# Column blocks of eight with bias tables in the same order, and the head order of the attention stage

## The chip, the cores and the metric

One core of one Trainium2 chip runs the whole program. The metric is the device time of one execution in microseconds (us). An instruction is named by its engine: PE is TensorE (matmuls and transposes), DVE is VectorE, ACT is ScalarE, POOL is GpSimd, and SP only issues DMAs. All data is float32.

## The reference: what is computed

512 tokens of width 1024 on a grid of 8 rows and 64 columns pass two layers. A layer is:

```
proj = x @ w_in                      # six blocks of 512: diff q, k, v and neighbourhood q, k, v
8 differential heads:  s_m = q_m k_m^T / sqrt(32) + t5_bias[bucket(key - query)],  m = 0, 1
                       o = (softmax(s_0) - lam * softmax(s_1)) @ v;  rms_norm(o) * g * (1 - lam_init)
8 neighbourhood heads: s = q k^T / 8 + rpb[row offset, column offset], only the 16 nearest columns
                       o = softmax(s) @ v
x = layer_norm(alpha * x + concat(o) @ w_out)
x = layer_norm(alpha * x + peer_ffn(x))      # product-key retrieval over 16384 experts
```

The result is x, (1, 512, 1024). With 8 grid rows the neighbourhood window covers all rows, so a neighbourhood head is limited in columns alone.

## The kernel before

`build` makes constants (`setup`), then runs a hardware loop over the two layers: `project`, `attend`, and three stages for the PEER part (`route`, `gates`, `experts`), which the change does not touch. A last block stores x.

**Token order.** x lies in SBUF as four tiles of 128 tokens (`per["x"][:, tt, :]`). Tile tt holds 16 grid columns of all 8 rows; inside it the column is the slow index and the row the fast one (`column_tokens`). Queries and keys have this order in every later stage.

**Project** (L361 on). Twelve half blocks j of `w_in` are loaded by SP into two buffers, split by ACT (L446) and DVE (L480) into a high and a low part, and multiplied on PE in three passes (L236 to L238); two result tiles n = 2j, 2j+1 come from each. ACT moves each tile out (L455, L463). The first eight tiles (q and k of the differential heads) also go to DRAM by SP (`store`, L412), and ACT may move tile n out only when the store of tile n-2 has landed. SP also copies the neighbourhood bias table 128 times to a DRAM scratch (L406) and loads the T5 table `tb` (L435): row p of `tb[:, h]` is the T5 bias of head h over 560 (row, column) offsets, cut so that the 512 entries that a query tile needs are one window of it. They come out of a scratch, filled once by ACT's queue in `setup` (L314).

**Attend** (L539 on). A unit u is one head for one query tile: 4 tiles of 16 heads, 64 units. A differential unit has two maps of 512 keys, a neighbourhood unit one map of 256. Each unit passes
- PE: scores into one of 4 PSUM banks (L864), three units ahead;
- DVE `maxima`: adds the bias, writes the negated sum to SBUF and keeps its minimum, in one instruction per map (L773);
- ACT: exponential with the row sum (L726);
- DVE `mix`, one unit behind: reciprocal, factor, and the weighted difference of the two maps (L784, L786, L789), differential units only;
- PE `turn`: transposes into the one bank Tb (L875); ACT `move`: Tb to SBUF (L736), two units behind; PE `values`: times v into O (L890), two units behind.

Every engine has its own instruction list, written out by `with_tails`: `unit(u)` for each u, and after unit 16*qt + slot the pieces of the **tail** of query tile qt. The tail reads O, normalises the differential heads (read_diff, gain), transposes them (turn_na, turn_diff), multiplies by w_out in four parts of 8 matmuls (mul_0 to mul_3, L934), adds to x (add_0, add_1, L833) and does the layer norm (stats, norm; L274 to L286). The slots decide where in the lists of the next tile's units these pieces stand. Only half of w_out fits: after mul_1, SP loads the other half (L645), and mul_2 waits for it. Limits between units: PB = 3 buffers of probabilities (maxima of u waits for turn of u-3), SB = 4 score banks, one bank Tb.

The order of heads is `mixed_order`: differential heads 0 to 5 (first tile) or 0 and 1 (others), then neighbourhood and differential heads in turn, then the neighbourhood heads left. The bias reads in L773 are

```
bias = tb[:, h, first:first + T].rearrange("p (r c) -> p c r", r=GR)
keys, bias = NKEYS, nb[:, EDGE[qt], h - NDH, :, :].rearrange("p r c -> p c r")
```

so the elements read one after the other lie 64 (T5) or 32 (neighbourhood) elements apart.

## Time and profile before

| | us |
|---|---|
| median of 3 runs (3435.12 to 3437.94) | 3437.25 |
| profiled execution, device time | 3439.33 |
| profiled execution, span | 3437.4 |
| PE busy | 3186.5 |
| DVE busy | 2554.2 |
| ACT busy | 1213.5 |
| POOL busy | 1083.8 |

The span is that of the recorded instructions; the device time holds 1.9 us more around it. Busy times are sums over the execution; engines overlap. A share of busy time says nothing of one stage, so the stages that the change touches are read from windows of the trace.

### The profile page before, as it was taken

The numbers are of one execution on the slowest core, as the hardware profiler recorded it, in microseconds if no ns is written. First come the engines' busy times: TensorE is split into PE (matmuls) and PEld (weight loads), VectorE is DVE, ScalarE is ACT, GpSimd is POOL, SyncE is SP. The second block draws the span as 40 slices with busy tenths as digits, with TensorE's granted clock in tenths as the row PEclk, the third lists the DMA queues.
The fourth block names the chain that finished last, engine by engine and source line by source line (L and its number), as shares of the span: only waits on it lengthen the run. The fifth ranks groups of instructions, "written<-read, shape, count | busy, mean of one in ns | idle before, by whom it ended". The sixth has DMA issues, their size and how long they took to land. (4 is left out here: it accounts for less than half of the span.)

```text
span 3437.4 us, 48720 instructions
## 1 busy us (share of the span) xinstructions
PE 3186.5 (93%) x16726; PEld 2820.0 (82%) x16726; DVE 2554.2 (74%) x5128; ACT 1213.5 (35%) x1716; POOL 1083.8 (32%) x684
## 2 busy tenths in 40 slices
PE   7988799899899999999889877998998999999997
PEld 6865489899899999988777664898998999999886
DVE  3186488899688878878832773898996888887787
ACT  2254233344333333333322551333443333332332
POOL 0020036500255545533200200474003555454332
PEclk9988899999999999999989898999999999999998
DMA  7541224446899999989675312244549999998995
GB/s 263 135 112 47 98 76 149 158 183 237 314 347 347 348 327 335 320 301 356 239 219 128 102 35 100 87 169 143 220 194 353 350 349 336 329 343 294 328 352 212
DMA packets 333656, 801.99 MB, mean 233 GB/s; under 512 B 39072, under 2 KB 195232, under 8 KB 298944
## 3 DMA queue, kind: packets, MB, share of 16 engines
q1 hardware_dynamic: 258736, 527.47, 44.7%
q0 software_dynamic: 73728, 268.47, 20.8%
q10 hardware_dynamic: 1040, 4.19, 0.3%
q8 instruction: 74, 1.21, 0.2%
q14 instruction: 78, 0.64, 0.1%
HBM read 711.45 MB, written 94.90 MB: 235 GB/s over the span
## 5 line engine op out<-in xcount | busy, mean ns | idle before, releaser
L236 PE MATMUL o_bank<-v_hi,w_hi 128*128 128x512 f32 x1536 | 599.6, 390 | 15.5 <-DVE w_lo L1580 15.5
L173 POOL DMA_INDIRECT g_ring<-in_peer_u,g_idx x256 | 361.6, 1412 | 796.6 <-DVE g_ring L183 747.3
L238 PE MATMUL o_bank<-v_hi,w_lo 128*128 128x512 f32 x1536 | 600.3, 391 | 0.0
L237 PE MATMUL o_bank<-v_lo,w_hi 128*128 128x512 f32 x1536 | 600.3, 391 | 0.0
L173 POOL DMA_INDIRECT g_ring<-in_peer_v,g_idx x256 | 372.3, 1454 | 505.9 <-DVE x_sb L191 449.9
L236 PE MATMUL h_bank<-x_hi,ws_hi 128*128 128x384 f32 x1152 | 385.7, 335 | 4.5 <-PEq L1248 4.5
L238 PE MATMUL h_bank<-x_hi,ws_lo 128*128 128x384 f32 x1152 | 385.7, 335 | 0.0
L237 PE MATMUL h_bank<-x_lo,ws_hi 128*128 128x384 f32 x1152 | 385.3, 334 | 0.0
L1565 DVE TENSOR_TENSOR v_lo<-v_raw,v_hi 128x2048 fp32r<-128x2048 f32 x128 | 292.8, 2288 | 123.8 <-ACT v_hi L1500 123.8
L183 DVE SCALAR_TENSOR_TENSOR g_ring<-g_ring,x_sb 128x1024 f32<-128x1024 f32 x256 | 306.4, 1222 | 99.3 <-DMA g_ring<-in_peer_u,g_idx 98.4
L1500 ACT CAST v_hi<-v_raw 128x2048 fp32r<-128x2048 f32 x128 | 244.9, 1913 | 375.2 <-PE o_bank L238 341.5
L191 DVE SCALAR_TENSOR_TENSOR x_sb<-g_ring,g_h,x_sb 128x1024 f32<-128x1024 f32 x256 | 328.3, 1282 | 58.3 <-DMA g_ring<-in_peer_v,g_idx 40.7
L236 PEld LDWEIGHTS o_bank<-v_hi,w_hi 128*128 128x128 f32 x1536 | 289.4, 188 | 74.6 <-issue 16.1
L238 PEld LDWEIGHTS o_bank<-v_hi,w_lo 128*128 128x128 f32 x1536 | 289.2, 188 | 60.6
L237 PEld LDWEIGHTS o_bank<-v_lo,w_hi 128*128 128x128 f32 x1536 | 289.4, 188 | 59.0
L236 PE MATMUL r_bank<-x_hi,ws_hi 128*128 128x384 f32 (+1 forms) x768 | 275.5, 359 | 12.5 <-DVE x_lo L267 12.5
L1180 POOL TENSOR_TENSOR ws_lo<-ws_raw,ws_hi 128x2048 fp32r<-128x2048 f32 x44 | 203.2, 4618 | 242.7 <-ACT ws_hi L1028 242.7
L237 PE MATMUL r_bank<-x_lo,ws_hi 128*128 128x384 f32 (+1 forms) x768 | 272.4, 355 | 0.0
L238 PE MATMUL r_bank<-x_hi,ws_lo 128*128 128x384 f32 (+1 forms) x768 | 272.2, 354 | 0.0
L1309 DVE TENSOR_SCALAR onehot<-iota,key1T,gateT 128x128 f32<-128x128 f32 x768 | 214.2, 342 | 33.3 <-PE g_bank L1340 26.0
L1340 PE MATMUL g_bank<-onehot 128*128 128x128 f32 x1536 | 208.5, 279 | 26.5 <-DVE onehot L1312 26.5
L1340 PEld LDWEIGHTS g_bank<-onehot 128*128 128x128 f32 x1536 | 199.5, 194 | 35.6 <-DVE onehot L1312 33.4
(190 smaller groups left out, 6118.5 us busy)
## 6 DMA issues: line engine op xcount, KB each, us to landing
ws_raw<-in_uT SPq DMA_DIRECT2D x128, 1024.0 KB
v_raw<-in_peer_v SPq DMA_DIRECT2D x128, 1024.0 KB
gates_T<-gate_stage SPq DMA_DIRECT2D x12, 4096.0 KB, 12.6
g_raw<-gates_T SPq DMA_DIRECT2D x128, 384.0 KB
w_raw<-in_w_in SPq DMA_DIRECT2D x24, 1024.0 KB, 6.3
ws_raw<-hidden_T SPq DMA_DIRECT2D x56, 384.0 KB
w_out_half<-in_w_out SPq DMA_DIRECT2D x8, 2048.0 KB, 8.1
ws_raw<-in_peer_wq SPq DMA_DIRECT2D x16, 1024.0 KB
```

Source lines behind the costliest of these rows:

```text
L173: nc.gpsimd.indirect_dma_start(out=tail.ring[n % RING][:, :], out_offset=None, in_=table.rearrange("l e d -> (l e) d"), in_offset=bass.Ind ...
L183: nc.vector.scalar_tensor_tensor(row, row, 1.0, xt, ALU.mult, ALU.mult, accum_out=tail.h[:, bass.ds(base + j, 1)]).then_inc(tail.used, 1)
L191: nc.vector.scalar_tensor_tensor(xt, tail.ring[j % RING][:, :], tail.h[:, bass.ds(base + j, 1)], xt, ALU.mult, ALU.add).then_inc(tail.used, 1)
L236: nc.tensor.matmul(out, lh, rh, start=start, stop=False)
L237: nc.tensor.matmul(out, lh, rl, start=False, stop=False)
L238: return nc.tensor.matmul(out, ll, rh, start=False, stop=stop)
L1180: nc.gpsimd.tensor_tensor(wl[n % 2][:, :, :], raw[n % 2][:, :, :], wh[n % 2][:, :, :].bitcast(F32), ALU.subtract).then_inc(lo_done, 1)
L1309: nc.vector.tensor_scalar(A[u % 2][:, t, :], iota[:, :], key1[:, bass.ds(col, 1)], gate[:, bass.ds(col, 1)], ALU.is_equal, ALU.mult)
L1340: ins = nc.tensor.matmul(bank[u % 4][:, t * NK:(t + 1) * NK], A[u % 2][:, t, :], B[u % 2][:, t, :], start=True, stop=True)
L1500: nc.scalar.copy(v_hi[k][:, :, :], v_raw[k][:, :, :]).then_inc(v_split, 1)
L1565: nc.vector.tensor_tensor(v_lo[k][:, :, :], v_raw[k][:, :, :], v_hi[k][:, :, :].bitcast(F32), ALU.subtract).then_inc(v_ready, 1)
```

## The change

- Tokens of a tile are now two blocks of 8 columns: block, then row, then column inside the block. Constants, the load of x and the store of the result follow; each of the 4 loads and 4 stores becomes two, of 64 partitions each.
- The T5 tables are laid out so that the 512 biases of a query tile lie one behind the other: SP loads the rows as before (2 DMAs instead of 8), and ACT copies them at the end of `project` (8 copies of 896 elements). The fill of the T5 scratch moves from `setup` to ACT's queue in `project` (after tile pair j = 1), so it is done in each layer. The neighbourhood tables are built by POOL in blocks of 64 elements. L773 now reads both tables block by block.
- The copy of the neighbourhood table to DRAM becomes two DMAs with 8 as their outermost dimension (16 before).
- Every tile runs its differential heads first (units 0 to 7) and then its neighbourhood heads (8 to 15), and all slots of the tail change.
- In the tail, the squares for the norm of the heads go from DVE to ACT, the gain g is applied by ACT while it moves the transposed heads, and the layer norm takes its sum from the add and its squares from ACT in place of the two statistics instructions on DVE.

```diff
+CB = 8
+TB = TC // CB
+T5_PITCH = CB * REL + GW - CB
+T5_W = (2 * GW - TC) * GR
+T5_RAW = NDH * (T5_W - TBW) + TBW
...
-    cq = np.arange(P) // GR
+    cq = np.arange(P) // (GR * CB) * CB + np.arange(P) % CB
...
+def column_tokens(t, n, g):
+
+    return at(t, (n * TC + g * CB) * D, [[GW * D, GR], [D, CB], [1, D]])
+
+
+def block_rows(g):
+
+    return slice(g * (P // TB), (g + 1) * (P // TB))
...
-                sp.dma_start(per["x"][:, tt, :], column_tokens(a["x"], tt)).then_inc(x_in, 16)
+                for g in range(TB):
+                    sp.dma_start(per["x"][block_rows(g), tt, :], column_tokens(a["x"], tt, g)).then_inc(x_in, 16)
...
-        @block.scalar
-        def _(act):
-            act.wait_ge(vec_made, 2)
-            nc.scalar.dma_start(at(t5_scratch, 0, [[NDH * REL, P], [REL, NDH], [1, REL]]),
-                                per["t5_vec"][:, None, :].to_broadcast([P, NDH, REL])).then_inc(t5_stored, 16)
...
-            sp.dma_start(at(rpb_scratch, 0, [[GR * RPC + 1, TC], [RPC + RPW, GR], [1, NNH * DRS * RPW]]),
-                         at(a["na_rpb"], l * (NNH * DRS * RPW), [[0, TC], [0, GR], [1, NNH * DRS * RPW]]))\
-                .then_inc(rpb_copied, 16)
+            for g in range(TB):
+                sp.dma_start(at(rpb_scratch, g * (GR * CB * RPC + CB),
+                                [[CB * RPC + RPW, GR], [RPC + 1, CB], [1, NNH * DRS * RPW]]),
+                             at(a["na_rpb"], l * (NNH * DRS * RPW), [[0, GR], [0, CB], [1, NNH * DRS * RPW]]))\
+                    .then_inc(rpb_copied, 16)
...
-                    for h in range(NDH):
-                        src = at(t5_scratch, h * P * REL + (T - 1) - (TT - 1) * TC,
-                                 [[GR * REL - 1, TC], [REL - GW, GR], [1, TBW]])
-                        sp.dma_start(tb[:, h, :], src).then_inc(tab_in, 16)
-            sp.wait_ge(tab_in, 16 * NDH)
+                    rows_first = tb[:, T5_RAW:T5_RAW + NDH * TBW].rearrange("p (h w) -> p h w", h=NDH)
+                    for g in range(TB):
+                        src = at(t5_scratch, (T - 1) - (TT - 1) * TC + g * (GR * T5_PITCH - CB),
+                                 [[REL - 1, GR * CB], [TB * GR * T5_PITCH, NDH], [1, TBW]])
...
+                if j == 1:
+                    nc.scalar.dma_start(at(t5_scratch, 0, [[T5_PITCH, P], [REL, CB], [1, REL]]),
+                                        per["t5_vec"][:, None, :].to_broadcast([P, CB, REL])).then_inc(t5_stored, 16)
+                if j == HALVES - 2:
+                    act.wait_ge(tab_in, 16 * TB)
+                    for h in range(NDH):
+                        first = T5_RAW + h * TBW
+                        if h >= 1:
+                            act.wait_ge(tab_made, h)
+                        nc.scalar.copy(tb[:, h * T5_W:(h + 1) * T5_W].rearrange("p (g r c) -> p g r c", r=GR, c=CB),
+                                       blocks_of_rows(tb, first)).then_inc(tab_made, 1)
...
+def blocks_of_rows(tb, first):
+
+    whole = tb[:, first:first + TBW]
+    return bass.AP(whole.tensor, whole.offset, [whole.ap[0], [CB, T5_W // (GR * CB)], [GW, GR], [1, CB]])
...
-        ORDERS = [mixed_order(6 if qt == 0 else 2) for qt in range(TT)]
+        ORDERS = [list(range(NH))] * TT
...
-        PE_SLOTS = {"turn_na": 20, "turn_diff": 23, "mul_0": 26, "mul_1": 27, "mul_2": 30, "mul_3": 31}
-        ACT_SLOTS = {"turn_na": 22, "turn_diff": 25}
-        DVE_SLOTS = {"read_diff": 18, "read_na": 20, "gain": 21, "add_0": 30, "add_1": 35, "stats": 37, "norm": 39}
-        POOL_SLOTS = {"read_diff": 18, "stats": 37}
-        SP_SLOTS = {"mul_1": 27}
+        PE_SLOTS = {"turn_diff": 15, "turn_na": 18, "mul_0": 20, "mul_1": 21, "mul_2": 23, "mul_3": 24}
+        ACT_SLOTS = {"square": 11, "turn_diff": 16, "turn_na": 19, "spread": 26}
+        DVE_SLOTS = {"read_diff": 11, "sums": 12, "gain": 14, "read_na": 18, "add_0": 22, "add_1": 25, "spread": 27,
+                     "norm": 28}
+        POOL_SLOTS = {"sums": 12, "spread": 27}
+        SP_SLOTS = {"mul_1": 21}
...
+                if piece == "square":
+                    act.wait_ge(o_read[0], qt + 1)
+                    if qt >= 1:
+                        act.wait_ge(spread, qt)
+                    nc.scalar.activation(sq, cat[:, 0:NDH, :], ACT.Square).then_inc(squared, 1)
                 if piece in ("turn_na", "turn_diff"):
                     i = 0 if piece == "turn_diff" else 1
-                    act.wait_ge(cat_turned, 2 * qt + (2 - i))
-                    if qt >= 1:
-                        act.wait_ge(hid, 2 * qt)
-                    nc.scalar.copy(catT[:, 4 * i:4 * i + 4, :].rearrange("p a b -> p (a b)"),
-                                   tail_bank(qt, 1 - i)[:, :]).then_inc(cat_moved, 1)
+                    act.wait_ge(cat_turned, 2 * qt + (i + 1))
+                    dst = catT[:, 4 * i:4 * i + 4, :].rearrange("p a b -> p (a b)")
+                    if i == 0:
+                        act.wait_ge(rms_asked, qt + 1)
+                        nc.scalar.activation(dst, tail_bank(qt, 0)[:, :], ACT.Copy,
+                                             scale=gd[:, 0:1]).then_inc(cat_moved, 1)
+                    else:
+                        if qt >= 1:
+                            act.wait_ge(spread, qt)
+                        nc.scalar.copy(dst, tail_bank(qt, 1)[:, :]).then_inc(cat_moved, 1)
+                if piece == "spread":
+                    act.wait_ge(centred, qt + 1)
+                    nc.scalar.activation(catT[:, :, :].rearrange("p a b -> p (a b)"), x[:, qt, :], ACT.Square,
+                                         bias=mv[:, 0:1], accum_out=mv[:, 1:2]).then_inc(spread, 1)
 
...
-                        keys, first = T, (TT - 1 - qt) * TC
-                        bias = tb[:, h, first:first + T].rearrange("p (r c) -> p c r", r=GR)
+                        keys, first = T, h * T5_W + (TT - 1 - qt) * P
+                        bias = tb[:, first:first + T]
+                        by_block = lambda t: t
                     else:
                         dve.wait_ge(nb_ready, h - NDH + 1 if qt == 0 else NNH + EDGE[qt])
-                        keys, bias = NKEYS, nb[:, EDGE[qt], h - NDH, :, :].rearrange("p r c -> p c r")
-                    by_column = lambda t: t.rearrange("p (c r) -> p c r", r=GR)
-                    nc.vector.tensor_tensor_reduce(by_column(s[u % PB][:, k, 0:keys]),
-                                                   by_column(S[(before + k) % SB][:, 0:keys]), bias, -1.0,
+                        keys, bias = NKEYS, nb[:, EDGE[qt], :, h - NDH, :, :].rearrange("p g r c -> p g (r c)")
+                        by_block = lambda t: t.rearrange("p (g k) -> p g k", k=GR * CB)
+                    nc.vector.tensor_tensor_reduce(by_block(s[u % PB][:, k, 0:keys]),
+                                                   by_block(S[(before + k) % SB][:, 0:keys]), bias, -1.0,
...
-                if piece == "read_diff":
-                    dve.wait_ge(o_read[0], qt + 1)
-                    if qt >= 1:
-                        dve.wait_ge(hid, 2 * qt)
-                    chain.done(nc.vector.tensor_tensor(sq, d, d, ALU.mult))
-                    chain.wait()
+                if piece == "sums":
+                    dve.wait_ge(squared, qt + 1)
                     chain.done(nc.vector.tensor_reduce(ms[:, 0, :], sq, AX_X, ALU.add))
                     chain.wait()
                     nc.vector.tensor_scalar(ms[:, 0, :], ms[:, 0, :], 1.0 / HD, EPS, ALU.mult,
                                             ALU.add).then_inc(rms_asked, 1)
                 if piece == "gain":
                     dve.wait_ge(rms_done, qt + 1)
-                    chain.done(nc.vector.tensor_tensor(d, d, ms[:, 1, :, None].to_broadcast([P, NDH, HD]), ALU.mult))
-                    chain.wait()
-                    nc.vector.tensor_tensor(d, d, gd[:, None, :].to_broadcast([P, NDH, HD]),
+                    nc.vector.tensor_tensor(d, d, ms[:, 1, :, None].to_broadcast([P, NDH, HD]),
                                             ALU.mult).then_inc(cat_done, 1)
...
-                                                   ALU.add).then_inc(x_done, 1)
-                if piece == "stats":
+                                                   ALU.add, accum_out=st[:, i:i + 1]).then_inc(x_done, 1)
+                if piece == "add_1":
+                    dve.wait_ge(x_done, 2 * (qt + 1))
+                    nc.vector.tensor_scalar(mv[:, 0:1], st[:, 0:1], st[:, 1:2], -1.0 / D, ALU.add,
+                                            ALU.mult).then_inc(centred, 1)
+                if piece == "spread":
+                    dve.wait_ge(spread, qt + 1)
+                    nc.vector.tensor_scalar(rs[:, 0:1], mv[:, 1:2], 1.0 / D, EPS, ALU.mult,
+                                            ALU.add).then_inc(pow_asked, 1)
+                if piece == "norm":
                     dve.wait_ge(ln_in, 32)
-                    dve.wait_ge(x_done, 2 * (qt + 1))
-                    norm_stats(nc, chain, xt, st, mv, rs[:, 0:1], pow_asked)
-                if piece == "norm":
-                    norm_apply(nc, dve, chain, xt, mv, lnp[:, 0, :], lnp[:, 1, :], rs[:, 1:2], pow_done, qt + 1)
+                    dve.wait_ge(centred, qt + 1)
+                    chain.done(nc.vector.scalar_tensor_tensor(xt, xt, mv[:, 0:1], lnp[:, 0, :], ALU.add, ALU.mult))
+                    chain.wait()
+                    dve.wait_ge(pow_done, qt + 1)
+                    chain.done(nc.vector.scalar_tensor_tensor(xt, xt, rs[:, 1:2], lnp[:, 1, :], ALU.mult, ALU.add))
 
...
-                sp.dma_start(column_tokens(out, tt), per["x"][:, tt, :]).then_inc(written, 16)
-            sp.wait_ge(written, 16 * TT)
+                for g in range(TB):
+                    sp.dma_start(column_tokens(out, tt, g), per["x"][block_rows(g), tt, :]).then_inc(written, 16)
+            sp.wait_ge(written, 16 * TT * TB)
```

## Rows read from the trace of the kernel before

**Rows 1.** Window of one period: length, busy of PE, PEld, DVE, ACT, POOL; PE clock, DMA.
```profile
287.30:342.40 55.10, 45.64 (x221) 33.94 (x219) 38.38 (x92) 25.05 (x66) 3.81 (x4) 0.85 0.16 48
```
**Rows 2.** PE in time, third query tile: start, length, form, idle before.
```profile
299.23 3.60 PE L934 MATMUL Hb<-w_out_half,heads_outT 128*128 128x512 f32 x8
...
304.38 3.60 PE L934 MATMUL Hb<-w_out_half,heads_outT 128*128 128x512 f32 x8
...
316.46 5.84 PE L934 MATMUL Hb<-w_out_half,heads_outT 128*128 128x512 f32 x8 [4.51 <-DMA w_out_half<-in_w_out]
...
323.63 3.60 PE L934 MATMUL Hb<-w_out_half,heads_outT 128*128 128x512 f32 x8
...
354.55 3.79 PE L934 MATMUL Hb<-w_out_half,heads_outT 128*128 128x512 f32 x8
```
**Rows 3.** DVE groups by line and shape: count, busy us, mean ns, idle before.
```profile
L773 DVE CUSTOM_DVE_ANT_1 probs<-S,t_toeplitz 128x512 f32<-128x512 f32 x128 | 128.4, 1045 | 54.6 <-PE S L864 46.8 <-PE Tb L875 7.6
...
L773 DVE CUSTOM_DVE_ANT_1 probs<-S,na_bias 128x256 f32<-128x256 f32 x64 | 38.2, 597 | 59.5 <-PE Tb L875 59.3
...
L496 DVE SCALAR_TENSOR_TENSOR q_diff_parts<-p_bank,q_diff_parts 128x512 fp32r<-128x512 f32 x16 | 11.1, 692 | 59.3 <-ACT q_diff_parts L455 59.3
```
**Rows 4.** DVE in time, second tile: mix of one unit, next unit's first map.
```profile
242.49 0.16 DVE L784 RECIPROCAL map_factor<-rowsum 128x1 f32<-128x1 f32 x1 [0.36 <-ACT probs L726]
...
243.61 1.02 DVE L773 CUSTOM_DVE_ANT_1 probs<-S,t_toeplitz 128x512 f32<-128x512 f32 x1
```
**Rows 5.** PE in time, one differential unit at full clock, one matmul group at half clock.
```profile
239.70 1.00 PE L890 MATMUL O<-dv,probsT 128*128 128x64 f32 x8
240.54 0.60 PE L875 MATMUL Tb<-ident,probs 128*128 128x128 f32 x4
240.90 0.72 PE L864 MATMUL S<-k_diff_parts,q_diff_parts 128*128 128x512 f32 x2
241.45 0.55 PE L890 MATMUL O<-nv_half_shifted,probsT 128*128 128x64 f32 x4
...
283.63 1.81 PE L890 MATMUL O<-dv,probsT 128*128 128x64 f32 x8
```
**Rows 6.** ACT group of the squares in `experts`.
```profile
L1551 ACT ACTIVATE ws_raw<-x_sb,bn_mv 128x1024 f32<-128x1024 f32 x6 | 6.9, 1151 | 23.0 <-DVE bn_mv L1648 23.0
```
**Rows 7.** DVE in time: first map of the stage, first map of the second tile.
```profile
172.72 1.05 DVE L773 CUSTOM_DVE_ANT_1 probs<-S,t_toeplitz 128x512 f32<-128x512 f32 x1 [23.35 <-PE S L864]
...
212.61 1.06 DVE L773 CUSTOM_DVE_ANT_1 probs<-S,t_toeplitz 128x512 f32<-128x512 f32 x1 [1.39 <-PE Tb L875]
```
**Rows 8.** PE in time, end of the attention stage: last turn, last products.
```profile
377.78 0.39 PE L875 MATMUL Tb<-ident,probs 128*128 128x128 f32 x2
...
389.64 8.51 PE L934 MATMUL S<-w_out_half,heads_outT 128*128 128x512 f32 x16 [0.77 <-ACT heads_outT L750]
397.99 7.03 PE L934 MATMUL S<-t_toeplitz,heads_outT 128*128 128x512 f32 x16
```
**Rows 9.** DVE in time, last instruction of the attention stage.
```profile
409.27 1.28 DVE L286 SCALAR_TENSOR_TENSOR x_sb<-x_sb,ln_rs,ln_params 128x1024 f32<-128x1024 f32 x1 [0.53 <-POOL ln_rs L698]
```
**Rows 10.** Window in the load of x, columns as in rows 1.
```profile
10.00:12.00 2.00, 0.00 (x0) 0.00 (x0) 0.00 (x0) 0.00 (x0) 0.00 (x0) 1.00 1.03 233
```
**Rows 11.** ACT in time, start of `project` in the first and in the second layer.
```profile
13.83 1.28 ACT L260 ACT_TABLE_LOAD   x1 [13.83 <-PEq L291]
...
25.84 1.90 ACT L446 CAST w_hi<-w_raw 128x2048 fp32r<-128x2048 f32 x1 [6.87 <-DMA w_raw<-in_w_in]
...
1725.25 1.28 ACT L260 ACT_TABLE_LOAD   x1 [10.70 <-issue]
...
1733.18 1.90 ACT L446 CAST w_hi<-w_raw 128x2048 fp32r<-128x2048 f32 x1 [1.91 <-DMA w_raw<-in_w_in]
```
**Rows 12.** SP's issues at the end.
```profile
3428.16 4.39 SPq L1778 DMA_DIRECT2D out<-x_sb  x4
```
**Rows 13.** DMA issues by line: count, KB each, median us to landing.
```profile
rpb_rows<-in_na_rpb SPq DMA_DIRECT2D x2, 3840.0 KB, 16.7
```

73 lines of the change are left out of this document (39 added, 34 removed).

## The prediction

> **What bounds the kernel now.** I read the page first: PE is busy nearly all the span, but the edits lie in the load of x, `project`, `attend` and the store, so the windows come next. In `attend` [rows 1] no engine is full: of a period of 55.10 us PE is busy 45.64 and DVE 38.38. The timeline then shows what a period is made of [rows 2]. From mul_0 (299.23) to the end of mul_3 (323.63 + 3.60) it is 28.0 us, and there PE sets the pace: four blocks of eight matmuls, and a wait of 4.51 us for the second half of w_out, after which mul_2 takes 5.84 us where the others take 3.60. The other 27.3 us, to the next mul_0 at 354.55, are DVE's: mixed pairs and the DVE pieces of the tail. A saving on DVE can thus show only in the second half of a period, in the first tile, and at the end.
>
> **The map instruction.** A T5 map takes 1.045 us for 512 elements, a neighbourhood map 0.597 for 256 [rows 3]. The difference is 1.75 ns an element, the start cost 0.15 us. L496 also reads PSUM and SBUF and writes SBUF, 512 elements one behind the other, in 0.692 us. I take that for the new T5 map (-0.35) and 0.15 + 256 x 1.06 ns = 0.42 for the other (-0.18). The bounds are L496's time and no change at all. The whole is 128 x 0.35 + 64 x 0.18 = 56 us of DVE work; the next parts ask how much of it shows. The Trainium skill (Advanced Engine Details and Errata, SBUF Cachelines) says that SBUF has lines of 16 bytes and that a new line for each access is penalised; by it the 256-byte step is what costs, and the new read is free of it.
>
> **A differential unit** on DVE: mix is 242.49 to 243.61, 1.12 us [rows 4], two maps 2 x 0.61 (0.69 less the overlap with the next start), so 2.35 us; before 3.05. On PE the unit is 0.84 + 0.36 + 0.55 = 1.75 us from the starts in [rows 5]; at half clock the O group takes 1.81 in place of 1.00, and the unit about 3.5.
>
> **A period after**, with time 0 where mul_0 starts (after unit 20):
> - mul_0 to 3.4, unit 21 to 5.1, mul_1 to 8.5. DVE's add_0 stands in slot 22 and waits for mul_1, with the maps of unit 23 and mix of 22 queued behind it. PE needs that mix for turn 22, and gets it at 8.5 + 0.7 + 1.2 + 1.1 = 11.5: it idles 1.7 us.
> - Units 22 and 23 end at 13.6. The half of w_out lands as late after mul_1 as before (307.8 to 316.46, 8.65 us [rows 2]), at 17.2. The wait is 3.6 us where it was 4.51, since two units lie in front of it where three did, but one of them was late. mul_2 5.84, unit 24 1.6, mul_3 3.4: 28.0 us, as before. That half gains nothing.
> - Then add_1 and the sum to 29.0; ACT squares x, 1.15 us [rows 6] plus 0.19 for the read of the sum, behind the exponential of unit 26; DVE waits for it in `spread` until 31.6, then read_diff 0.9, both norm instructions 2.6, sums 0.9: 36.3. POOL's power (1.65) and gain: 38.7. The neighbourhood units 28 to 31 wait for DVE meanwhile, then go through Tb at some 1.1 us each: turn 31 at 41.9. Five differential units at 2.35: turn 36 at 54.2.
> - Clock: in the period before it was 0.85 of full [rows 1]. PE is now idle for about half of the stretch 29 to 42, so the first differential units behind it will meet the half clock, where PE (3.5) and not DVE (2.35) sets the unit. I add 1.8: a period of 56.0 against 55.3. Three tails lie over units: +2 us a layer. Bounds: 54.2 (-3) and three more units at half clock a tile (+12).
> So most of the DVE saving is lost: units are no longer mixed, so the DVE-heavy and the latency-bound ones do not cover each other.
>
> **The first tile** took 39.9 us (172.72 to 212.61 [rows 7]). After: eight differential units in 23.5 (18.8 by DVE; PE at half clock in the first four, POOL's building of tables beside the mixes), eight neighbourhood units at 1.1, and 3.5 for the DVE pieces in slots 11 to 14: 36. That is -4, bounds 0 and -7.
>
> **The end of the stage** took from the last turn (377.78 + 0.39) to 409.27 + 1.28 [rows 8, 9] 32.4 us, with mul_3 of the third tile and the whole differential tail behind the turn. Now both lie before it. What is left: two values 1.3, read_na 0.9, transposes and their move 1.1, the 32 matmuls 15.4 [rows 8], add and mean 1.0, square 1.3, power and scaling 1.7, last norm 1.3, signals 1: 25. That is -7, bounds -9 and -4.
>
> Attention: 2 x (+2 - 4 - 7) = **-18 us**.
>
> **Load of x.** While it runs all DMA engines are full (1.03) at 233 GB/s [rows 10]: 9.0 us for 2.1 MB. The transfers were 16 rows outermost over 128 partitions and are 8 rows outermost over 64. No row shows an outermost dimension of 8. If it changes nothing, 0; if 8 engines carry it, 18.0 us, +9.0. I take the upper end: full engines leave nothing else to give. Against it the 4 MB store of the T5 scratch leaves this place: in the first layer w_in came 12.0 us after the block's start, in the second, without that store beside it, 7.9 [rows 11]: -4.1. Net +4.9.
> **Store of x.** It runs from 3428.16 to the end of the span at 3437.4 [rows 12], 9.2 us for the same 2.1 MB. Bounds 0 and +9; I take +7, doubling all but the latency of the last.
> **Project.** The copy of the table takes 16.7 us to land [rows 13] with w_in, stores and all else of SP's queue behind it; doubled, it delays the moves of tiles n = 2, 3 and with them the split for j = 3, which has about 6 us to spare in the first layer and less in the second. The T5 store comes right behind on ACT's queue. Bounds 0 and +10 a layer, I take +1: +2. The eight copies by ACT (some 1.0 us each) lie between moves that are 5.2 us apart on an idle ACT and end before the last matmul: 0; uncovered they would be 8 a layer. Building the tables on POOL: same elements, 0.
>
> Sum against the profiled execution: 3439.3 - 18 + 4.9 + 7 + 2 = 3435.2; the median of the runs is 2.1 below that execution, so **3433 us**.
>
> The Trainium skill (DMA: Bandwidth & Descriptors, Why a DMA increments its semaphore by 16 and not by 1) says that a transfer runs on the largest number of engines up to 16 that divides the slowest dimension of both sides, 8 here. By it the forecast stands; without it, the first rival.
>
> **Rivals.**
> - Transfers as fast as before. For it: no row at 8 against it; full engines may be full with waiting. Then 9.0, 7 and 2 fall away: 3415. Chance 0.25.
> - The clock. PE idles in the neighbourhood run and is then held at half clock through most of the differential run: 1.15 us more for each of 8 to 9 units a layer: +10 a layer, 3453, slower. It decides once more than about 5 of the 20 differential units behind the tails and in the first tile beyond those I count are at half clock. For it: 0.85 mean clock in a period that had shorter gaps [rows 1]. Against: PE is full while it is slow, as in mul_2, after which it ran at 3.60 again. Chance 0.18.
> - The map stays at 1.045 us: the instruction, not its read, is slow. Then the some 21 differential units a layer that DVE paces cost 0.7 more: +15 a layer, 3463, slower. No row shows this instruction on a contiguous bias. Chance 0.07.
> - The periods come out at the full-clock sum, 54.2: 3422. Chance 0.08.
>
> **How the numbers follow.** The forecast has 0.42, with 3424 to 3443 as its own range. A measurement of this kernel tells 0.2% (7 us) from no change, so faster is below 3430. Of the forecast's chance 0.15 is faster, 0.21 the same, 0.06 slower. With the rivals: faster 0.15 + 0.23 + 0.07 = 0.45; same 0.21 + 0.02 + 0.01 = 0.24; slower 0.06 + 0.18 + 0.07 = 0.31. The range 3410 to 3456 leaves out the third rival and the edges.
>
> **What would show it.** L773 at about 0.69 and 0.42 us. First transposes of the first layer near 22 us, not 14, and the windows before them with half the DMA share. From mul_0 to mul_3's end 28 us, with 1.7 us of PE idle between unit 22's values and its turn. Periods near 56, the first tile 36, last turn to last norm 25 us. From the first store issue to the end 16 us. Wrong: a period below 53 or above 59, or loads that land as before.

## The result and the profile after

The changed kernel takes **3461.2 us** (median of four runs, 3460.4 to 3461.9) where the kernel before takes 3437.6: ratio 1.007, 95% interval 1.0057 to 1.0082. It is slower; 3433 had been forecast. The profiled executions have spans of 3459.5 and 3437.4 us, and the 22.1 us between them divide so ("attend" is from SP's first q load to the end of the last norm instruction, "project" from the start of the layer's work to that load):

| | before | after | difference | forecast |
|---|---|---|---|---|
| setup and project, layer 0 | 168.5 | 173.7 | +5.1 | +5.9 |
| attend, layer 0 | 242.0 | 244.1 | +2.1 | -9 |
| project, layer 1 | 150.3 | 154.1 | +3.8 | +1 |
| attend, layer 1 | 240.0 | 244.2 | +4.2 | -9 |
| both expert parts | | | -0.3 | 0 |
| store of x | 9.2 | 16.5 | +7.2 | +7 |

The first row looks like its forecast, but by luck. PE's first matmul with w_in stands at 27.6 us, 31.3 before, so the head of the layer is 3.7 us shorter, where 4.9 longer had been forecast; from there to the first q load it takes 146.1 us, 137.2 before, 8.9 longer, where 1 had been forecast.

The maps are as fast as forecast. The groups of DVE by line and shape, after, against [rows 3]:

```profile
L821 DVE CUSTOM_DVE_ANT_0 probs<-S,t_tables 128x512 f32<-128x512 f32 x128 | 82.8, 686 | 64.2 <-PE S L915 46.7 <-PE Tb L926 17.3
...
L821 DVE CUSTOM_DVE_ANT_1 probs<-S,na_bias 128x256 f32<-128x256 f32 x64 | 25.9, 419 | 5.2 <-PE Tb L926 5.0
```

That is 1045 to 686 ns and 597 to 419 ns, 57 to 58 us less work for DVE. The next two fences are one window each over attend of layer 0 (columns as in [rows 1]: length, busy PE, PEld, DVE, ACT, POOL, clock, DMA share, GB/s), before and then after:

```profile
168.54:410.55 242.01, 187.10 (x864) 134.92 (x864) 158.06 (x356) 100.60 (x264) 38.16 (x40) 0.84 0.26 75
```

```profile
173.66:417.75 244.09, 185.63 (x864) 134.44 (x864) 121.91 (x348) 102.15 (x276) 37.92 (x40) 0.86 0.26 75
```

DVE is busy for 36 us less, and the stage is 2 us longer. The first place where the saving is lost is the end of the first tile. PE in time, after:

```profile
216.26 1.22 PE L915 MATMUL S<-k_diff_parts,q_diff_parts 128*128 128x512 f32 x2 [5.80 <-DMA q_diff_parts<-diff_qk_parts]
217.27 0.95 PE L941 MATMUL O<-nv,probsT 128*128 128x64 f32 x4
```

PE wants the q of tile 1 and waits 5.80 us for it. SP's issues in time, after, say why it is late:

```profile
188.07 0.98 SPq L699 DMA_DIRECT2D nv_half_shifted<-nv  x1
189.09 0.60 SPq L700 DMA_DIRECT2D nv_half_shifted<-nv  x1
204.03 0.38 SPq L675 DMA_DIRECT2D w_out_half<-in_w_out  x1
204.60 0.44 SPq L703 DMA_DIRECT2D ln_params<-in_ln_g  x1
205.14 0.38 SPq L704 DMA_DIRECT2D ln_params<-in_ln_b  x1
205.57 9.66 SPq L671 DMA_DIRECT2D q_diff_parts<-diff_qk_parts  x16
```

SP stands from 189.7 to 204.03 at its wait for POOL's last table, because w_out goes into the buffer that POOL reads. POOL's row ends at 203.87:

```profile
191.99 11.88 POOL L740 TENSOR_TENSOR na_bias<-w_out_half,win_mask 128x256 f32<-128x256 f32 x9 [0.56 <-DMA w_out_half<-rpb_rows]
```

The q loads, which need none of that, are queued behind it and behind 3 MB of other loads. The kernel before had the same list, 30.4 us from first q load to w_out load there as here. But its tile took 39.9 us, so that q came 0.6 us late; now the tile could be done in 35 and meets the full wait. The wait is there in layer 1 too, 5.0 us. DVE's first maps of tile 0 and of tile 1, against [rows 7]:

```profile
177.85 0.69 DVE L821 CUSTOM_DVE_ANT_0 probs<-S,t_tables 128x512 f32<-128x512 f32 x1 [23.37 <-PE S L915]
...
218.69 0.69 DVE L821 CUSTOM_DVE_ANT_0 probs<-S,t_tables 128x512 f32<-128x512 f32 x1 [6.87 <-PE Tb L926]
```

The first tile took 40.8 us. The periods, against [rows 2]:

```profile
294.41 3.60 PE L985 MATMUL Hb<-w_out_half,heads_outT 128*128 128x512 f32 x8
...
311.23 5.43 PE L985 MATMUL Hb<-w_out_half,heads_outT 128*128 128x512 f32 x8 [1.33 <-DMA w_out_half<-in_w_out]
...
350.46 3.60 PE L985 MATMUL Hb<-w_out_half,heads_outT 128*128 128x512 f32 x8
```

The period from 236.82 to 294.41 took 57.6 us and the next 56.05, against 55.9 and 55.3 before. The end of the stage, from the last turn to the last norm, is 390.81 to 417.75 = 26.9 us, against 32.4 in [rows 8, 9].

In project PE has a wait that it did not have before:

```profile
125.29 0.80 PE L246 MATMUL p_bank<-xh_p,w_hi 128*128 128x512 f32 x1 [6.91 <-DVE w_lo L502]
```

And x moves on half of the engines, as the DMA shares of 0.52 and 0.49 have it. A window of the store before comes first, then a window of the load, SP's issue and a window of the store after, against [rows 10, 12]:

```profile
3431.00:3434.00 3.00, 0.00 (x0) 0.00 (x0) 0.00 (x0) 0.00 (x0) 0.00 (x0) 0.50 1.03 401
```

```profile
10.00:12.00 2.00, 0.00 (x0) 0.00 (x0) 0.00 (x0) 0.00 (x0) 0.00 (x0) 1.00 0.52 213
...
3443.04 10.68 SPq L1828 DMA_DIRECT2D out<-x_sb  x8
...
3448.00:3453.00 5.00, 0.00 (x0) 0.00 (x0) 0.00 (x0) 0.00 (x0) 0.00 (x0) 0.50 0.49 165
```

### The profile page after: what moved, and what is told of

It reads as the page before. It is cut to its first block and busy times, and to the rows that moved or that the text cites. A ratio compares the mean times of both kernels' runs of the same rounds, so it can differ in the third digit from the quotient of the medians.

```text
span 3459.5 us, 48751 instructions
## 1 busy us (share of the span) xinstructions
PE 3192.4 (92%) x16726; PEld 2826.6 (82%) x16726; DVE 2482.3 (72%) x5112; ACT 1233.9 (36%) x1756; POOL 1091.7 (32%) x684
## 3 DMA queue, kind: packets, MB, share of 16 engines
q0 software_dynamic: 73728, 268.47, 20.7%
## 5 line engine op out<-in xcount | busy, mean ns | idle before, releaser
L246 PEld LDWEIGHTS o_bank<-v_hi,w_hi 128*128 128x128 f32 x1536 | 289.4, 188 | 74.8 <-issue 16.2
L246 PE MATMUL r_bank<-x_hi,ws_hi 128*128 128x384 f32 (+1 forms) x768 | 275.3, 358 | 11.1 <-DVE x_lo L277 11.1
L1391 PE MATMUL g_bank<-onehot 128*128 128x128 f32 x1536 | 208.4, 279 | 26.9 <-DVE onehot L1363 26.9
```

Source lines behind the costliest of these rows:

```text
L246: nc.tensor.matmul(out, lh, rh, start=start, stop=False)
L1391: ins = nc.tensor.matmul(bank[u % 4][:, t * NK:(t + 1) * NK], A[u % 2][:, t, :], B[u % 2][:, t, :], start=True, stop=True)
```

## The experiments

Each was timed against the kernel before on the same chip. Times are medians; the ratio with its 95% interval stands beside.

### The wait in the first tile: q_early

```diff
-            sp.wait_ge(nb_ready, NNH + 2)
-            load_wo(wo[:, :, :], half(0, 0))
-            sp.dma_start(lnp[:, 0, :], at(a["ln1_g"], l * D, [[0, P], [1, D]])).then_inc(ln_in, 16)
-            sp.dma_start(lnp[:, 1, :], at(a["ln1_b"], l * D, [[0, P], [1, D]])).then_inc(ln_in, 16)
...
                         load_q(u // NH + 1, head(u) // 2)
+                    if u == LAST_DIFF[0]:
+                        sp.wait_ge(nb_ready, NNH + 2)
+                        load_wo(wo[:, :, :], half(0, 0))
...
```

> The changed kernel, but in SP's list for attend the wait for the neighbourhood tables, the first half of w_out and the two ln1 rows stand behind the q load of unit 7 instead of ahead of all q loads. Theory 1 (part of the loss is this wait of the first tile: PE idles 5.80 us at 216.26 for q_diff_parts, and then runs at half clock): the row loses its 5.80, the first tile goes from 40.8 to about 34.5, and two layers give 12 to 14 us: 3447 to 3449. Theory 2 (the first tile is held by DVE and the latency of unmixed units, the wait only stands where another would): under 3 us in all, 3458 or more. Rival to both: w_out now comes too late for mul_0 of tile 0 (issued near 205 instead of 204, needed at 236): no.

**3449.3 us**, 1.0034 (1.0022 to 1.0046): 12 us back. Theory 1 holds. SP's issues in q_early:

```profile
189.03 10.35 SPq L671 DMA_DIRECT2D q_diff_parts<-diff_qk_parts  x16
203.43 0.40 SPq L675 DMA_DIRECT2D w_out_half<-in_w_out  x1
```

The first tile is 35.2 us (176.60 to 211.77). Attend is 237.3 and 236.3 us, so the wait and what hung on it had cost 7 to 8 us a layer. The periods stay at 56.2 to 57.1.

### The stalls in project: t5_setup, rpb_16

t5_setup takes the T5 store out of project and lets ACT issue it once, in setup. rpb_16 has the old copy of the bias table:

```diff
 t5_setup, in setup (and the same issue taken out of project)
+            act.wait_ge(vec_made, 2)
+            nc.scalar.dma_start(at(t5_scratch, 0, [[T5_PITCH, P], [REL, CB], [1, REL]]), ...
 rpb_16
-            for g in range(TB):
-                sp.dma_start(at(rpb_scratch, g * (GR * CB * RPC + CB),
-                                [[CB * RPC + RPW, GR], [RPC + 1, CB], [1, NNH * DRS * RPW]]),
...
+            sp.dma_start(at(rpb_scratch, 0, [[GR * RPC + 1, TC], [RPC + RPW, GR], ...
```

> The changed kernel, but the 4 MB T5 store is issued once, by ACT in setup, as in the kernel before, and not in each project. Theory 1 (the store in project delays w_in and the stores of the parts: PE idles about 6.9 us in the first layer and 5.5 in the second for the low part of w_in): the second layer's project falls from 154.1 to 149 to 151 and the first one's by 5 to 7, of which the start gives back 2 to 4: 3452 to 3455. Theory 2 (the stall is the table copy on half of the engines, the T5 store only lies behind it): 3461 to 3465, with both stalls in place.

> The changed kernel, but the copy of the bias table to its scratch is one transfer with 16 outermost, as in the kernel before (the scratch then has the old row order, so the neighbourhood bias differs; timing only). Theory 1 (halved engines for this copy delay what stands behind it): PE's stalls in project shrink from 6.9 and 5.5 us to under 2, 3449 to 3453. Theory 2 (the T5 store causes them): 3458 to 3462.

t5_setup **3451.0**, 1.0041 (1.0027 to 1.0055); rpb_16 **3444.8**, 1.0021 (1.0012 to 1.0030), more than expected. In both PE has no wait for w_lo left in either layer's project, where the changed kernel has 6.9 and 5.5 us. So neither theory holds alone: the stall needs both, the 4 MB store and a copy on half of the engines beside it. Its size is not fixed: the six other runs with both (q_early, q_early_slots, mixed, map_strided, x_rows16, tables_alone) wait 3.4 to 5.7 us in layer 0 and 2.8 to 5.2 in layer 1 (q_early has the 3.4 and the 2.8). The head of the first layer pays in t5_setup: PE's first transposes stand at 23.0 us, 16.5 in the changed kernel.

### The order: mixed

```diff
-        ORDERS = [list(range(NH))] * TT
+        ORDERS = [mixed_order(6 if qt == 0 else 2) for qt in range(TT)]
...
-        PE_SLOTS = {"turn_diff": 15, "turn_na": 18, "mul_0": 20, "mul_1": 21, "mul_2": 23, "mul_3": 24}
+        PE_SLOTS = {"turn_diff": 22, "turn_na": 25, "mul_0": 27, "mul_1": 28, "mul_2": 30, "mul_3": 31}
...
+        DVE_SLOTS = {"read_diff": 17, "read_na": 18, "sums": 19, "gain": 21, "add_0": 30, "add_1": 33, "spread": 34,
+                     "norm": 36}
```

> The changed kernel with its tables and new tail pieces, but differential and neighbourhood heads mixed as in the kernel before, and the pieces in slots near the old ones (turn_diff 22, turn_na 25, mul_0 27 to mul_3 31, add_1 33, norm 36). Theory 2 (the order ate the map's saving): periods of 50 to 53 us in place of 56 to 57.6, the first tile no longer waits for q, the end of the stage is back at about 30 from 26.9; attend falls from 244.5 to 228 to 235 a layer, 3440 to 3448 in all, though transfers are as slow as in the changed kernel. Theory 1 (the transfers and the q wait are the whole loss, the order is neutral): only the q wait goes, 3447 to 3450, with periods of 55 to 57.

**3475.2**, 1.0104 (1.0088 to 1.0121), 14 us slower than the changed kernel, which neither theory had. This said nothing on the order yet, since the slots were mine: DVE stood 14.0 to 14.2 us at add_1 in each period. It is taken up again below.

### Later adds: q_early_slots

```diff
-        DVE_SLOTS = {"read_diff": 11, "sums": 12, "gain": 14, "read_na": 18, "add_0": 22, "add_1": 25, "spread": 27,
-                     "norm": 28}
+        DVE_SLOTS = {"read_diff": 11, "sums": 13, "gain": 14, "read_na": 18, "add_0": 23, "add_1": 27, "spread": 29,
+                     "norm": 30}
```

> The kernel of q_early, with DVE's add_0 in slot 23 (from 22), add_1 in 27 (from 25), spread and norm in 29 and 30, ACT's square in 12 and spread in 28; PE's slots are untouched. In q_early DVE stands 21.8 us of a period at the adds while ACT waits 26.7 us for row maxima. Theory 3 (the adds stand too early in DVE's list, and the maps of three or four units behind them come too late for the time after mul_3): periods fall from 56 to 57 to 52 to 54, that is 3 to 4 us for each of six, 3425 to 3432. Rival (PE between mul_0 and mul_3, and DVE's own work after it, set the period whatever the order of the adds; before had them late and took 55.3): within 4 us of q_early, 3445 to 3453.

**3452.4**, 1.0051 (1.0036 to 1.0066), no better than q_early; periods 56.7 to 58.2. Theory 3 fell. From the second mul_0 to the third DVE now waits 8.7 us at the adds, where q_early has 21.8, but 15.2 us for PE's transposes, where q_early has 1.0. So DVE waits as long as before in another place; why the period does not shrink is argued from this, not shown by a run of its own.

### What the map is worth: map_strided, before_contig

```diff
 map_strided, in the changed kernel
-                        bias = tb[:, first:first + T]
+                        bias = tb[:, first:first + T].rearrange("p (r c) -> p c r", r=GR)
 before_contig, in the kernel before
-                        bias = tb[:, h, first:first + T].rearrange("p (r c) -> p c r", r=GR)
+                        bias = tb[:, h, first:first + T].rearrange("p (c r) -> p c r", r=GR)
```

> The changed kernel, with the T5 table read in steps of 64 elements again (scores and output too in that order, so a differential head's bias is of another pair; timing only), 128 maps. Theory (the read's step alone makes the instruction slow, and some part of its 45 us of DVE work shows): L821's 512 form at 1.04 us, and attend longer by 12 to 20 us a layer, 3485 to 3500; this is what the table order saves in the new head order. Rival (it was hidden beside PE and latency): attend longer by under 4 us a layer, 3461 to 3469.

> The kernel before, with one line changed: a differential head's bias is read from the T5 table as 512 neighbouring elements in place of steps of 64 (the bias is then of another pair; timing only). 128 maps should take 0.69 us in place of 1.045. Theory 4 (in the mixed order most of the saving is hidden, since PE or the w_out wait sets half of each period; the new order gets no less from it, as map_strided showed 14 us there): 3422 to 3432. Rival (the mixed order with its late adds gets more of it, the new order is the loss): 3405 to 3418. No change (3434 or more) would say that DVE paces nothing in the mixed order.

map_strided **3475.2**, 1.0113 (1.0098 to 1.0127), 14 us above the changed kernel; the group of its maps:

```profile
L821 DVE CUSTOM_DVE_ANT_1 probs<-S,t_tables 128x512 f32<-128x512 f32 x128 | 127.9, 1042 | 53.3 <-PE S L915 46.8 <-PE Tb L926 6.4
```

before_contig **3419.6**, 0.9955 (0.9942 to 0.9969), 16.5 us under its own kernel before, with periods of 51.3 us and attend at 231.9 and 232.3. The step of the read alone makes the map slow (686 ns with that one line changed), as the Trainium skill's rule has it (Advanced Engine Details and Errata, SBUF Cachelines: a new cacheline for each access is penalised). Of 45 to 46 us of DVE work 14 show in the new order and 16.5 in the old one: about a third in both. But the old order with fast maps has periods of 51.3 us in layer 0 and 51.5 to 53.1 in layer 1, the new one of 56 to 58. And the 16.5 us are not all that the faster map can give in the old order. before_contig still has the q loads behind w_out, and now pays for it as the changed kernel does, 5.2 us here and 5.6 in layer 1, where before had 0.6 and 1.0:

```profile
208.88 1.22 PE L864 MATMUL S<-k_diff_parts,q_diff_parts 128*128 128x512 f32 x2 [5.16 <-DMA q_diff_parts<-diff_qk_parts]
```

### x on 16 engines, small copies, two queues: x_rows16, dma_spread

```diff
 x_rows16, and the same for the store
-                for g in range(TB):
-                    sp.dma_start(per["x"][block_rows(g), tt, :], column_tokens(a["x"], tt, g)).then_inc(x_in, 16)
+                sp.dma_start(per["x"][:, tt, :], plain_tokens(a["x"], tt)).then_inc(x_in, 16)
 dma_spread, behind load(j) for j = 4 to 11, g = n % TB, c = n // TB * 2, n = j - 4
+                sp.dma_start(at(rpb_scratch, g * (GR * CB * RPC + CB) + c * (RPC + 1),
+                                [[CB * RPC + RPW, GR], [RPC + 1, 2], [1, NNH * DRS * RPW]]), ...
 dma_spread, in the store
+                nc.scalar.dma_start(column_tokens(out, tt, 1), per["x"][block_rows(1), tt, :]).then_inc(written_a, 16)
```

> The changed kernel, with x loaded and out stored in the old order of tokens, one transfer a tile with 16 outermost over 128 partitions (tokens then don't sit beside their bias; timing only). Theory 1 (8 outermost puts the transfer on half of the engines): from the first store issue to the end 9 to 9.5 us instead of 16.5, the block of project starts 1 to 3 us earlier than 16.35, 3451 to 3454. Rival (the number of transfers or their wait costs, not their outer size): the store loses under 2 us, 3458 to 3461.

> The changed kernel with the q loads of q_early, the T5 store of t5_setup, the bias table's copy cut in eight transfers of 480 KB, one behind each of the loads of w_in for j = 4 to 11, and the output stored half by SP's queue and half by ACT's. Theory 1: q_early's 12 and t5_setup's 10 us add up, and the small copies hold nobody up: 3437 to 3441; the last transfers share the same half of the engines whoever issues them, so the store still takes 16 to 16.5 us. Rival for the store (the half of the engines is the queue's, not the shape's): 10 to 11 us, and 3431 to 3435. Rival for the copies (they come too late or delay each w_in load): project of layer 1 stays above 152 us and the whole at 3442 or more.

x_rows16 **3448.4**, 1.0033 (1.0021 to 1.0046): 13 us back, more than expected. The store took 9.2 us again (3437.73 to 3446.9), PE's first transposes stood at 14.2 us (16.5), and the wait in project of layer 0 was shorter too (4.7 us in place of 6.9), which is within what other runs show with x on half of the engines. dma_spread **3461.3**, 1.0069 (1.0057 to 1.0082): its attend was 237 as in q_early, but the first q load came 7.7 us later than in the changed kernel and project of layer 1 took 6.0 us more (160.0), so all of the gain was lost. SP's issues of the copies took up to 10.9 us each, and w_in stood behind them. ACT's queue did not help the store: 17.7 us.

### Healed versions: fixed, all_16, fixed_pool_x

fixed has the edits of q_early and t5_setup, all_16 those of rpb_16 and x_rows16 besides. fixed_pool_x adds to fixed, in the load and likewise in the store:

```diff
+            for tt in range(TT):
+                nc.gpsimd.dma_start(per["x"][block_rows(1), tt, :], column_tokens(a["x"], tt, 1)).then_inc(x_in1, 16)
```

> The changed kernel with the q loads of q_early and the T5 store of t5_setup, nothing else. If the two losses are apart: 3461 - 12 - 10 = 3439, the same as the kernel before within 0.2%. If they share something (with q_early alone one stall of the project stayed, with t5_setup alone layer 0's attend was already 4 us shorter): 3442 to 3445.

> The kernel of fixed, with x, out and the bias table's copy in their old form (16 outermost; x and bias then don't fit each other; timing only): what the change gives once none of its transfers is slower than before. Theory: fixed less x_rows16's 13 us and what is left of rpb_16's 16 (t5_setup has taken most of it): 3439 - 13 - 2 to 6, so 3420 to 3424, faster than before by 0.4 to 0.5%. Rival (something else in the new order is slower than before, and the transfers only cover it): 3430 or more.

> The kernel of fixed, with the second block of eight columns of x loaded, and of out stored, by GpSimd's queue. In dma_spread ACT's queue did not help SP's (17.7 us for the store). Theory (the shape alone chooses the engines, whatever queue): the store takes 16 to 18 us and the total is within 3 us of fixed. Rival (this queue makes its own descriptors and spreads them over other engines): the store falls to 10 to 13 us, and 3432 to 3436 in all.

fixed **3439.3**, 1.0007 (0.9997 to 1.0016): the losses add. all_16 **3426.9**, 0.9975 (0.9966 to 0.9984): with the transfers in their old form the change does gain, but only 9 us; attend is still 237.6 and 236.6. fixed_pool_x **3434.0**, 0.9997 (0.9988 to 1.0006). Its store took 14.0 us, and GpSimd's queue does reach the other engines. One window of the store each, of fixed, of fixed_pool_x, and of pool_copies (below), where GpSimd issues all of it:

```profile
3430.00:3435.00 5.00, 0.00 (x0) 0.00 (x0) 0.00 (x0) 0.00 (x0) 0.00 (x0) 0.50 0.51 166
```

```profile
3423.00:3428.00 5.00, 0.00 (x0) 0.00 (x0) 0.00 (x0) 0.00 (x0) 0.00 (x0) 0.50 0.90 218
```

```profile
3413.00:3417.00 4.00, 0.00 (x0) 0.00 (x0) 0.00 (x0) 0.00 (x0) 2.43 (x5) 0.50 0.91 271
```

The Trainium skill (DMA: Bandwidth & Descriptors, Why a DMA increments its semaphore by 16 and not by 1) has both halves of this: a transfer of 8 from SP's or ACT's queue goes to the lowest-numbered 8 engines, one from GpSimd's to 8 consecutive ones from a cursor that moves on. Shares of 0.51, 0.90 and 0.91 agree; which engines it was no view here shows.

### Order or pieces: mixed_old_tail, mixed_new_tail, new_order_old_tail

All three have the tables, the q loads, the T5 store and the x transfers of fixed_pool_x, and differ from it in the order of heads, in the tail pieces with their slots, or in both:

```diff
 mixed_old_tail: attend of the kernel before, with the changed kernel's masked(), maxima() and wo_end
 mixed_new_tail, against fixed_pool_x
-        sq = catT[:, 0:DC // 2, :].rearrange("p c (h d) -> p (c h) d", d=HD)
+        sq = per["t5_vec"][:, 0:NDH * HD].rearrange("p (h d) -> p h d", d=HD)
...
+        ORDERS = [mixed_order(6 if qt == 0 else 2) for qt in range(TT)]
+        PE_SLOTS = {"turn_diff": 21, "turn_na": 23, "mul_0": 26, "mul_1": 27, "mul_2": 30, "mul_3": 31}
+        DVE_SLOTS = {"read_diff": 17, "read_na": 18, "sums": 19, "gain": 20, "add_0": 30, "add_1": 35, "spread": 36,
+                     "norm": 38}
 new_order_old_tail, against mixed_old_tail
+        ORDERS = [list(range(NH))] * TT
+        PE_SLOTS = {"turn_na": 18, "turn_diff": 19, "mul_0": 20, "mul_1": 21, "mul_2": 23, "mul_3": 24}
+        DVE_SLOTS = {"read_diff": 11, "gain": 13, "read_na": 18, "add_0": 23, "add_1": 25, "stats": 26, "norm": 28}
```

> The kernel of fixed_pool_x (3434 us, attend 237.1 and 236.1) with the attend of the kernel before (mixed heads, its tail pieces and slots) on the new tables, q loads as in fixed. Theory (the new order or its pieces keep the period at 56, the tables give 51): attend 231 to 233 a layer, 3423 to 3427, faster than before by 0.3 to 0.4%. Rival (the contiguous read's gain in before_contig needed its fast transfers): 3430 or more.

> The kernel of fixed_pool_x with mixed heads and the new tail pieces, with the slots of the kernel before as near as can be (mul_0 26, mul_1 27, mul_2 30, mul_3 31, add_1 35, spread 36, norm 38; the squares go to a buffer of their own). In mixed the pieces were at 27 to 36 and a period took 57 to 58. Theory (order and slots decide, the pieces are neutral): attend 231 to 235, 3424 to 3431. Rival (the new pieces are slower in a mixed order, since ACT's square and DVE's wait for it stand in the way of the units): 3438 to 3450.

> The kernel of fixed_pool_x with the new order of heads but the old tail pieces (squares, sums and gain by DVE, bn_stats), mul_0 to mul_3 in the same slots. Theory (the order decides): periods of 56 to 59, at or above fixed_pool_x, 3434 to 3446; DVE has more to do in the stretch behind mul_3. Rival (the pieces decide): periods of 52 to 54, 3418 to 3428.

| | attend, both layers | us | ratio to before |
|---|---|---|---|
| new order, new pieces (fixed_pool_x) | 237.1, 236.1 | 3434.0 | 0.9997 (0.9988 to 1.0006) |
| mixed order, old pieces | 225.1, 226.5 | 3411.8 | 0.9926 (0.9912 to 0.9939) |
| mixed order, new pieces | 242.1, 239.9 | 3442.0 | 1.0014 (1.0005 to 1.0023) |
| new order, old pieces | 253.8, 250.0 | 3461.5 | 1.0072 (1.0058 to 1.0085) |

mixed_old_tail is 11 us below its theory, new_order_old_tail 15 us above anything that its two theories had; mixed_new_tail lies in its rival's range. Order and pieces together lose 22 us to what they replaced. Which of the two does it can't be said from the crossed versions, whose slots I chose: mixed_new_tail has read_diff so early that DVE stands 10.38 us for its O bank, and the clock in the second half of a period fell to 0.79 and 0.70 in the two (mixed_new_tail and new_order_old_tail). The half of a period from the end of mul_3 to the next mul_0, in fixed_pool_x and in mixed_old_tail:

```profile
311.08:339.94 28.86, 20.22 (x131) 17.75 (x131) 23.69 (x71) 19.70 (x55) 3.80 (x4) 0.94 0.00 1
```

```profile
313.30:337.03 23.73, 18.87 (x128) 17.14 (x128) 21.50 (x59) 15.35 (x42) 2.58 (x2) 0.93 0.00 1
```

The other half is 27.5 and 27.7 us; all of the difference is here, at the same clock. PE is idle for 8.6 us against 4.9, and DVE for 5.2 against 2.2. Idle time is not all of the 5.1 us: DVE also has 2.2 us more to do in this half (23.7 us in 71 instructions against 21.5 in 59), since the new order puts more of its work here and less into the other half (5.4 against 10.1). DVE's rows of fixed_pool_x in that stretch show the links of a chain, each waiting for another engine (the 13.88 us of the first lie in the other half, ahead of the stretch):

```profile
311.12 0.69 DVE L881 SCALAR_TENSOR_TENSOR x_sb<-x_sb,Hb 128x512 f32<-128x512 f32 x1 [13.88 <-PE Hb L991]
...
314.49 0.15 DVE L889 TENSOR_SCALAR ln_rs<-ln_mv 128x1 f32<-128x1 f32 x1 [1.72 <-ACT heads_outT L803]
...
320.91 1.09 DVE L874 TENSOR_TENSOR heads_out<-heads_out,heads_ms 128x512 f32<-128x512 f32 x1 [1.02 <-POOL heads_ms L730]
```

In mixed_old_tail the same stretch goes on without such waits between two maps; its longest wait is at the squares:

```profile
313.39 0.69 DVE L852 TENSOR_TENSOR heads_outT<-heads_out 128x512 f32<-128x512 f32 x1 [1.12 <-PE Hb L970]
```

### The tables alone, and the queue: tables_alone, pool_copies, pool_late

tables_alone is the changed kernel, transfers and T5 store and all, with the order, pieces and slots of before. pool_copies is mixed_old_tail with out stored and the bias table copied by GpSimd; pool_late lets that copy wait until both first blocks of w_in are split:

```diff
 pool_copies, in project (SP's copy taken out)
+            for g in range(TB):
+                nc.gpsimd.dma_start(at(rpb_scratch, g * (GR * CB * RPC + CB),
+                                       [[CB * RPC + RPW, GR], [RPC + 1, CB], [1, NNH * DRS * RPW]]), ...
...
+            nc.gpsimd.dma_reset(range(rpb_sem.num, rpb_sem.num + 1))
 pool_late, ahead of it
+            pool.wait_ge(hi_done, 2)
```

> The changed kernel with all its tables and transfers, but with the order of heads, tail pieces and slots of the kernel before. Theory (order and pieces lose 20 to 22 us, as between fixed_pool_x at 3434 and mixed_old_tail at 3412, and the q wait of 7 us a layer is small in this order, since before waited 0.63 us): 3461 less 22 less 10 to 14, so 3425 to 3431. Rival (the slow transfers also meet the mixed order's loads, or its first tile waits for q too): 3435 or more.

> The kernel of mixed_old_tail, with all of out stored by GpSimd's queue and the bias table's copy issued by GpSimd too. Theory (its queue uses other engines than the half that the shape gives on SP's; the DMA share in the store of fixed_pool_x was 0.90 where fixed had 0.51): store 10 to 12 us instead of 14, project 0 to 3 us shorter, 3 to 6 us under mixed_old_tail. Rival (only two queues beside each other fill the engines): store 15 us or more, the same time or up to 4 us slower.

> The kernel of pool_copies, with the bias table's copy held until both first blocks of w_in are split. Theory (the copy took the engines from the first w_in loads, which cost 12 us in layer 0): PE's first wait falls back from 20.8 to about 9, the store stays at 10.8 us, 3408 to 3412. Rival (the copy on this queue costs as much wherever it stands): 3418 to 3424.

tables_alone **3438.9**, 1.0008 (0.9998 to 1.0017): 22 us under the changed kernel by order and pieces alone, as in the table. It is not below before, since the rival had a part of it: in this order too SP's q loads come late. Its attend takes 232.0 and 233.0 us, where mixed_old_tail, with q loaded early, has 225.1 and 226.5: that is 6 to 7 us a layer for the queue's order, near the 7 to 8 in the new order of heads. PE's waits for q from 173 to 245 us (total, times, longest), of which the kernel before has 4.9, 2, 4.2:

```profile
PE S L894 <- DMA q_diff_parts<-diff_qk_parts: 9.1, 3, 4.5
```

pool_copies **3422.4**, 0.9960 (0.9946 to 0.9973): the store took 10.8 us, and project 12 us more, with PE waiting 20.8 us for its first x parts where mixed_old_tail has 9.3; neither theory had that. pool_late **3410.9**, 0.9924 (0.9910 to 0.9937): PE's first wait is 9.8 us, the store 10.9. It leaves nothing of the reference out, beats both kernels, and is the same within its interval as mixed_old_tail.

## Why the prediction was wrong

- **The map instruction**: right, 0.69 and 0.42 us.
- **The first tile**: this step failed. Forecast 36 us, measured 40.8. The 36 held for DVE and PE (35.2 in q_early), but the sum asked of SP's queue nothing. The q loads of tile 1 were issued 32 us behind the stage's start in both kernels, and only the slower tile had hidden them. With what follows from it this is 14.8 us of the two attends (244.1 and 244.2 against 237.3 and 236.3 in q_early). The attends missed their forecast by 24.3 us, and the whole sum missed the profiled execution by 26.2.
- **A period**: forecast 56.0, measured 56.0 to 57.6. From mul_0 to the end of mul_3 28.0 was forecast and 27.2 measured; the two waits I named were there, in other sizes (2.25 and 1.33 us for 1.7 and 3.6). The other half was 0.9 us longer than forecast. From the first map of tile 1 to the last turn q_early needs 171.0 us where before needed 165.6, +5.4 for the +2. Two steps of the working are also a little off as sums: 31.6 and its terms make 36.0 and not 36.3, and five units of 2.35 behind 41.9 end at 53.7 and not 54.2.
- **The end of the stage**: forecast 25, measured 26.9 (27.0 in q_early), so -5 and not -7.
- **That the order loses most of the saving**: right in sense, and it can be priced now: 22 us in all for order and pieces together, which of the two is open. It was one sentence with no rival of its own. The prediction took the mixed order as the frame for the costs and never asked what the same maps would give there.
- **The load of x**: two terms, each to be read from its own row. PE's first transposes tell when x has landed. They stand at 13.9 to 14.2 us in the four traces with 16 outermost, at 20.7 to 23.3 in the three with 8 outermost on SP's queue and the T5 store beside it (+8.3 in the mean), and at 16.2 to 21.3 (mean 18.4, +4.4) in the seven with the store moved away. So the +9.0 was an upper end, as the text said, and the changed kernel's profiled execution had one of the shortest, +2.5. Its premise, that full engines leave nothing else to give, did not hold there: half of them moved 213 GB/s where all had moved 233. The -4.1 was for w_in. From the first transposes to the first matmul with w_in it is 11.1 us, 17.4 before: -6.3. Together the head is -3.7 in that execution, and -1.8 in the mean of the seven, for the +4.9.
- **Project**: +1 a layer was forecast, +3.8 measured in layer 1 and +8.9 in layer 0, counted from the first matmul with w_in. The term named the copy and the T5 store "right behind" it, but did not ask what the two do together.
- **The store of x**: right, +7.2. There the engines had moved 401 GB/s before, and 165 on half of them.
- The rival "transfers as fast as before" would have given 3426.9 with the q loads healed (all_16), not 3415. The measured 3461 lies beside the 3463 of the rival on the map, but by chance, since the map ran in 0.69 us; and its price of +15 a layer was twice the 7 to 8 that map_strided shows (attend 251.9 and 251.3). The clock was no cause: 0.88 and 0.91 in the two periods, 0.85 and 0.88 before, and 0.86 against 0.84 in the stage.

## What to carry to other kernels

When an engine gets faster, ask of each queue what stands first in it at the new time: a load behind an unrelated wait is free only as long as the slower work hides it. A change that brings a faster instruction and a new order at once should be priced in halves, since here the instruction alone was worth 16.5 us, even with the q loads still behind w_out, and the order with its pieces cost 22. And when rows are regrouped, look at the outermost size of every transfer: 8 in place of 16 from SP's or ACT's queue halves the engines, and GpSimd's queue can take them instead.

## What the runs showed of the hardware

- Half of the engines do not take twice the time in each place, nor the same time in each execution. From 10 to 12 us in the load of x the full set moved 233 GB/s at a DMA share of 1.03; half of it moved 213 at 0.52 in the changed kernel, 209 in rpb_16, 160 in q_early and 131 in mixed, with the same setup code. Going out it was 165 at 0.49 against 401 at 1.03.
- The store of the T5 scratch did not delay x while x used all engines (13.9 us with it, 14.0 in all_16's 16-engine load, which has it too, and 14.2 in x_rows16 without it), but by some 4 us in the mean once x used half of them (three traces with it, 20.7 to 23.3; seven without, 16.2 to 21.3).
- With the table's copy on half of the engines and the T5 store beside it PE waited 3.4 to 6.9 us for the low part of w_in in layer 0 (seven traces); with either of them alone in that place it did not wait.
- With the same setup code the first transposes stood anywhere from 16.2 to 21.3 us. A part of the spread between the medians of such kernels can be this, so differences of 3 us between them are not read here.
